# Four picks of 32 tokens in each expert gather, sums in column quarters, and copies of rows made on TensorE

## The reference, cut to what matters

```python
qh = (xb @ wq).reshape(PEER_BLOCK, PEER_HEADS, 2, PEER_DKEY // 2)        # 8 heads, 2 halves of 128
s = jnp.einsum('thcd,hckd->thck', qh, keys)                              # 128 keys for each half
sv, si = lax.top_k(s, PEER_TOPK)                                         # 16 best of each half
cand = (sv[:, :, 0, :, None] + sv[:, :, 1, None, :]).reshape(PEER_BLOCK, PEER_HEADS, -1)
cidx = (si[:, :, 0, :, None] * PEER_NKEYS + si[:, :, 1, None, :]).reshape(PEER_BLOCK, PEER_HEADS, -1)
sc, pos = lax.top_k(cand, PEER_TOPK)                                     # 16 best of 256 pairs
eidx = jnp.take_along_axis(cidx, pos, axis=-1)                           # 0 .. 16383
gw = jax.nn.softmax(sc, axis=-1)
hpre = jnp.einsum('td,thkd->thk', xb, u_tab[eidx])                       # a gathered row of u, dotted
act = jax.nn.gelu(hpre, approximate=False) * gw
return jnp.einsum('thk,thkd->td', act, v_tab[eidx])                      # gathered rows of v, weighted and summed
```

## Time and profile before

| what | value |
|---|---|
| median of 3 runs | 5446.84 us (5442.61 to 5446.93) |
| the profiled execution's own time | 5444.57 us |
| its span, granted clock | 5442.9 us, 0.932 |
| busy over the span | PE 4506.8 us (83%), DVE 2595.2 (48%), ACT 1807.0 (33%), POOL 1616.7 (30%) |
| gathers of expert rows | 1056, 1 MB each |
| DMA bytes over the span | 1639.75 MB, mean 301 GB/s |

### The profile page before, as it was taken

How to read it: one execution, slowest core, us unless ns; L and a number is a source line. 1 busy time by engine, 2 the same in 40 slices (tenths; PEclk the granted TensorE clock), 3 DMA queues, 4 the chain that set the end, 5 groups by cost and what they waited for, 6 DMA issues and landing times.

```text
span 5442.9 us, 53986 instructions
## 1 busy us (share of the span) xinstructions
PE 4506.8 (83%) x17703; PEld 2724.5 (50%) x17703; DVE 2595.2 (48%) x5453; ACT 1807.0 (33%) x4693; POOL 1616.7 (30%) x1451
## 2 busy tenths in 40 slices
PE   7999999985665666799688888888888888888898
PEld 6888888875564644344333343343333333333352
DVE  3111111115636851122266666666666666666664
ACT  3111111113323531222144444444444444444434
POOL 0000000004535820100144444444444444444433
PEclk9999999996656887899899999999999999999989
DMA  7898988751114636622499999999999999999988
GB/s 254 281 305 267 305 270 283 246 191 61 62 47 145 171 136 263 238 85 71 154 421 421 421 421 421 421 421 420 419 419 412 417 415 416 415 415 406 415 335 367
DMA packets 312486, 1639.75 MB, mean 301 GB/s; under 512 B 39384, under 2 KB 83032, under 8 KB 170328
## 3 DMA queue, kind: packets, MB, share of 16 engines
q0 software_dynamic: 167344, 1179.45, 53.1%
q1 hardware_dynamic: 109472, 235.86, 12.6%
q10 hardware_dynamic: 35456, 221.91, 12.6%
HBM read 1550.80 MB, written 315.93 MB: 343 GB/s over the span
## 4 chain that ended last, share of the span: by engine, by line
DMA 34%; PE 13%; issue 2%; ACT 1%; DVE 0%; POOL 0%; SPq 0%; DVEq 0%; POOLq 0%; ACTq 0%; PEldq 0%
DMA ex_rows<-scratch_uv,ex_E 34%; PE ex_ps_y L2353 9%; PE ex_ps_q L2322 4%; ACT ex_diag L2149 1%; ACT ex_w L2141 0%; PE ex_ps_s L2335 0%; ACT ex_gel L2137 0%; POOL ex_rows L2101 0%; SPq L2062 0%; DVE ex_dots L2275 0%; DMA ex_wq<-in_peer_wq 0%; PE ex_ps_t L2295 0%; DVE ex_rows L2275 0%; ACT ex_keysT L2108 0%; PE ex_ps_t L2306 0%
## 5 line engine op out<-in xcount | busy, mean ns | idle before, releaser
L2353 PE MATMUL ex_ps_y<-ex_rows,ex_diag 128*128 128x512 f32 (+1 forms) x4224 | 2024.9, 612 | 405.2 <-ACT ex_diag L2149 386.2
L2275 DVE CUSTOM_DVE_ANT_0 ex_rows<-ex_rows,ex_n2u 128x1024 f32<-128x1024 f32 x1056 | 1294.1, 1225 | 940.6 <-DMA ex_rows<-scratch_uv,ex_E 931.0
L2101 POOL DMA_INDIRECT ex_rows<-scratch_uv,ex_E x1056 | 1154.7, 1093 | 1724.1 <-PE ex_ps_y L2353 1491.3
L2353 PEld LDWEIGHTS ex_ps_y<-ex_rows,ex_diag 128*128 128x128 f32 (+1 forms) x4224 | 728.4, 188 | 1604.6 <-ACT ex_diag L2149 939.6
L307 PE MATMUL pj_ps<-pj_w_hi,pj_nT 128*128 128x470 f32 (+1 forms) x3456 | 783.7, 378 | 22.5 <-PE pj_ps L307 14.4
L307 PEld LDWEIGHTS pj_ps<-pj_w_hi,pj_nT 128*128 128x128 f32 (+1 forms) x3456 | 622.3, 181 | 149.3 <-issue 32.0
L2137 ACT ACTIVATE ex_gel<-ex_dots 128x1 f32<-128x1 f32 x1056 | 213.8, 202 | 1368.2 <-DVE ex_dots L2275 1367.2
L211 DVE COPY pj_zo<-pj_ps 128x470 f32<-128x470 f32 (+1 forms) x108 | 69.7, 645 | 899.4 <-PE pj_ps L307 764.6
L2149 ACT ACTIVATE ex_diag<-ex_ident,ex_w 128x128 f32<-128x128 f32 x1024 | 411.0, 401 | 50.5 <-PE ex_ps_y L2353 17.7
L307 PE MATMUL pj_ps<-pj_w_lo,pj_nT 128*128 128x470 f32 (+1 forms) x1728 | 406.0, 377 | 0.0
L211 ACT COPY pj_zo<-pj_ps 128x470 f32<-128x470 f32 (+1 forms) x108 | 59.6, 552 | 996.5 <-PE pj_ps L307 622.2
(11 more groups left out here) (351 smaller groups left out, 3925.9 us busy)
## 6 DMA issues: line engine op xcount, KB each, us to landing
pj_w<-in_w_in POOLq DMA_DIRECT2D x24, 1880.0 KB, 14.5
scratch_z<-pj_zo SPq DMA_DIRECT2D x192, 235.0 KB, 8.7
scratch_uv<-in_peer_u ACTq DMA_DIRECT2D x8, 4096.0 KB, 21.0
scratch_uv<-in_peer_v ACTq DMA_DIRECT2D x8, 4096.0 KB, 38.1
scratch_uv<-in_peer_u ACTq DMA_DIRECT2D x4, 8192.0 KB, 38.1
scratch_uv<-in_peer_v ACTq DMA_DIRECT2D x4, 8192.0 KB, 69.0
out_dk_s<-in_cache_dil_k ACTq DMA_DIRECT2D x8, 4088.0 KB, 43.6
out_dv_s<-in_cache_dil_v ACTq DMA_DIRECT2D x8, 4088.0 KB, 55.9
```

Of the source, the lines that this page charges most:

```text
L2101: pool.indirect_dma_start(out=rows[:, p % SLOTS, :], out_offset=None, in_=d["uv"], in_offset=bass.IndirectOffsetOnAxis(ap=E[:, turn % 4, k ...
L2275: nc.vector.tensor_tensor_reduce(out=row, in0=row, in1=n2u[:, tile % 2], scale=1.0, scalar=0.0, op0=ALU.mult, op1=ALU.add, accum_out=dots[ ...
L2353: last = nc.tensor.matmul(y[0:n, 512 * c:512 * c + 512], diag[:, p % DIAGS, 0:n], rows[:, p % SLOTS, D + 512 * c:D + 512 * c + 512], start ...
```

## The change

A gather of a prompt turn now takes the picks 4q to 4q+3 of 32 tokens (group g = k % 4, q = k // 4): partition 32 j + t holds pick 4q + j of token 32 g + t. The routing still computes with one token on each partition, so its results (`own`) are spread: `spread_picks` multiplies them on TensorE with four matrices `copies4`, each of which copies 32 tokens to all four blocks of partitions, and `take_spread` on DVE picks the wanted columns into `spread` and E. The dots need each group's normalised rows four times: `copy_rows` makes them on TensorE from n2r and `take_copies` copies them on ACT to `n2u`, which has four buffers and is not loaded by DMA any more. The sums use the folded 128x32 matrix in all turns, as four products of 256 columns; the product of column quarter c is written to partitions 32 c to 32 c + 31 of ps_y (column group c of TensorE). So h and y are held by column quarters and moved in four DMAs with pieces of 1 KB. `ps_y` has one buffer, and `rows` 11 slots instead of 12.

```diff
-    SLOTS = 12
+    SLOTS = 11
+    G = P // NS
+    CW = D // G
...
+        copies4 = sb("copies4", [P, G, G, NS])
-        n2r, n2u, n2T = sb("n2r", [P, D]), sb("n2u", [P, 2, D]), sb("n2T", [P, KD, P])
-        h, yo = sb("h", [P, D]), sb("yo", [P, D])
+        n2r, n2u, n2T = sb("n2r", [P, D]), sb("n2u", [P, G, D]), sb("n2T", [P, KD, P])
+        h, yo = sb("h", [P, G, CW]), sb("yo", [P, G, CW])
...
-        ps_y, ps_t = pb("ps_y", [P, 2, D]), pb("ps_t", [P, KD, P])
+        ps_y, ps_t = pb("ps_y", [P, G, CW]), pb("ps_t", [P, KD, P])
...
+        def by_column(a, tile):
+            rows32 = a[tokens(tile), :] if tile is not None else a
+            return rows32.rearrange("(g t) (c e) -> c t g e", t=NS, c=G)
...
-            def load_u(tile):
...
+            def load_h(tile):
+                n = width(tile) // NS
+                for c in range(G):
+                    sp.dma_start(h[c * NS:(c + 1) * NS, 0:n], by_column(d["h"], tile)[c]).then_inc(h_in, 16)
...
                     sp.wait_ge(n2_t, tile + 1)
+                    sp.wait_ge(copied, G * (tile + 1))
                     sp.dma_start(n2r[0:width(tile + 1)], d["n2"][tokens(tile + 1), :]).then_inc(n2r_in, 16)
-                    load_u(tile + 1)
...
+            def take_copies(tile, g):
+                act.wait_ge(copied, G * tile + g + 1)
+                if tile:
+                    act.wait_ge(dot_done, K * first_of(tile) - G + g + 1)
+                nc.scalar.copy(n2u[:, g], ps_t[:].rearrange("p k t -> p (k t)")).then_inc(n2u_out, 1)
...
             for turn in range(3):
...
                 scores(turn)
+                if turn == 0:
+                    for g in range(G):
+                        take_copies(0, g)
                 if turn < 2:
                     exponents(turn)
...
+                    if k == 0 and turn and closes(turn - 1):
+                        outputs(tile_of(turn - 1))
                     weights(turn, k)
                     diagonal(turn, k)
+                    if turn < NT * PH and closes(turn) and k >= K - G and (k - K + G) * NS < width(tile_of(turn) + 1):
+                        take_copies(tile_of(turn) + 1, k - K + G)
...
+            def take_spread(turn):
+                dve.wait_ge(r_done, turn + 1)
+                src = ps_r[:].rearrange("p (g c q j) -> p g c q j", g=G, c=2 * G, q=G)
+                for j in range(G):
+                    at = slice(j * NS, (j + 1) * NS)
+                    into = spread[at, turn % 4].rearrange("p c (q g) -> p g c q", g=G)
+                    for c in range(2):
+                        nc.vector.tensor_copy(into[:, :, c], src[at, :, c, :, j]).then_inc(spread_done, 1)
+                dve.wait_ge(spread_done, 2 * G * (turn + 1))
+                nc.vector.tensor_copy(E[:, turn % 4], spread[:, turn % 4, 0]).then_inc(E_done, 1)
...
             for turn in range(2):
                 for part in range(K):
                     route(turn, part)
+                if turn == 0:
+                    take_spread(0)
             for turn in range(TURNS):
                 for k in range(K):
                     dot(turn, k)
+                    if k == 2 and turn + 1 < NT * PH:
+                        take_spread(turn + 1)
...
+            def copy_rows(tile, g):
+                n = width(tile)
+                if tile == 0 and g == 0:
+                    pe.wait_ge(copies4_done, 1)
+                pe.wait_ge(n2T_out, tile + 1)
+                if g:
+                    pe.wait_ge(n2u_out, G * tile + g)
+                for b in range(2):
+                    last = nc.tensor.matmul(ps_t[:, 4 * b:4 * b + 4].rearrange("p k t -> p (k t)"), copies4[0:n, g].rearrange("p j t -> p (j t)"),
+                                            n2r[0:n, 512 * b:512 * b + 512], start=True, stop=True)
+                last.then_inc(copied, 1)
...
+            def spread_picks(turn):
+                if turn == 0:
+                    pe.wait_ge(copies4_done, 1)
+                pe.wait_ge(own_done, turn + 1)
+                pe.wait_ge(gate_done, turn + 1)
+                if turn:
+                    pe.wait_ge(spread_done, 2 * G * turn)
+                for g in range(G):
+                    last = nc.tensor.matmul(ps_r[:, P * g:P * g + 2 * K], copies4[:, g].rearrange("p j t -> p (j t)"),
+                                            own[:, turn % 2].rearrange("p c k -> p (c k)"), start=True, stop=True)
+                last.then_inc(r_done, 1)
...
-                for c in range(2):
-                    last = nc.tensor.matmul(y[0:n, 512 * c:512 * c + 512], diag[:, p % DIAGS, 0:n],
-                                            rows[:, p % SLOTS, D + 512 * c:D + 512 * c + 512],
+                for c in range(G):
+                    last = nc.tensor.matmul(ps_y[c * NS:(c + 1) * NS, g], diag[:, p % DIAGS, :], rows[:, p % SLOTS, D + CW * c:D + CW * (c + 1)],
                                             start=False, stop=end, skip_group_check=True)
...
             for turn in range(3):
                 if opens(turn):
                     turn_rows(turn)
+                if turn == 2:
+                    spread_picks(0)
                 queries(turn)
                 scores(turn)
+                if turn == 0:
+                    for g in range(G):
+                        copy_rows(0, g)
             for turn in range(TURNS):
                 for k in range(K):
                     sum_row(turn, k)
+                    at = k - K + G + 1
+                    if turn < NT * PH and closes(turn) and at >= 0 and at * NS < width(tile_of(turn) + 1) and at < G:
+                        copy_rows(tile_of(turn) + 1, at)
+                    if k == 1 and turn + 1 < NT * PH:
+                        spread_picks(turn + 1)
```

More of the change, by code:

```diff
@@ L2157, in outputs @@
                 if tile:
-                    act.wait_ge(y_stored, 16 * tile)
-                n = width(tile)
-                nc.scalar.copy(yo[0:n], ps_y[0:n, tile % 2]).then_inc(y_done, 1)
+                    act.wait_ge(y_stored, 16 * G * tile)
+                n = width(tile) // NS
+                nc.scalar.copy(yo[:, 0:n], ps_y[:, 0:n]).then_inc(y_done, 1)
             for turn in range(3):
@@ L2179, in _ @@
                             scores(turn + 3)
-                    if k == 3 and turn and closes(turn - 1):
-                        outputs(tile_of(turn - 1))
                     if k == 8 and turn + 2 < TURNS:
@@ L2257, in route @@
                     dve.wait_ge(pick_done, turn + 1)
-                    nc.vector.scalar_tensor_tensor(out=e, in0=picked[:, 0], scalar=float(NKEY), in1=picked[:, 1],
-                                                   op0=ALU.mult, op1=ALU.add).then_inc(E_done, 1)
+                    if turn >= 2 and turn < NT * PH:
+                        dve.wait_ge(r_done, turn - 1)
+                    into, done = (mine[:, 0], own_done) if turn < NT * PH else (E[:, turn % 4], E_done)
+                    nc.vector.scalar_tensor_tensor(out=into, in0=picked[:, 0], scalar=float(NKEY), in1=picked[:, 1],
+                                                   op0=ALU.mult, op1=ALU.add).then_inc(done, 1)
                 elif part == 14:
@@ L2274, in dot @@
                 row = rows[:, p % SLOTS, 0:D]
-                nc.vector.tensor_tensor_reduce(out=row, in0=row, in1=n2u[:, tile % 2], scale=1.0, scalar=0.0, op0=ALU.mult,
+                nc.vector.tensor_tensor_reduce(out=row, in0=row, in1=n2u[:, g], scale=1.0, scalar=0.0, op0=ALU.mult,
                                                op1=ALU.add, accum_out=dots[:, turn % 2, k:k + 1]).then_inc(dot_done, 1)
@@ L2304, in turn_rows @@
                     pe.wait_ge(n2T_out, tile)
+                    pe.wait_ge(n2u_out, G * tile)
                 for k in range(KD):
@@ L2337, in scores @@
                 last.then_inc(s_done, 1)
+            def spread_picks(turn):
[9 more added lines that the diff above has]
+                last.then_inc(r_done, 1)
             def sum_row(turn, k):
-                p, tile = turn * K + k, tile_of(turn)
-                n, y = width(tile), ps_y[:, tile % 2]
+                p, tile, g = turn * K + k, tile_of(turn), group(turn, k)
                 if k == 0 and opens(turn):
-                    pe.wait_ge(h_in, 16 * (tile + 1))
-                    if tile >= 2:
-                        pe.wait_ge(y_done, tile - 1)
-                    for c in range(2):
-                        last = nc.tensor.matmul(y[0:n, 512 * c:512 * c + 512], ident[0:n, 0:n], h[0:n, 512 * c:512 * c + 512],
+                    pe.wait_ge(h_in, 16 * G * (tile + 1))
+                    if tile:
+                        pe.wait_ge(y_done, tile)
+                    for b in range(2 if tile < NT else 1):
+                        two = slice(2 * b, 2 * b + 2) if tile < NT else slice(0, 1)
+                        last = nc.tensor.matmul(ps_y[:, two].rearrange("p g e -> p (g e)"), ident[:], h[:, two].rearrange("p g e -> p (g e)"),
```

67 lines of the change are left out of this document (32 added, 35 removed).

## The result

The changed kernel takes 5466.2 us (median of 6 runs, 5462.57 to 5470.08) against 5445.91 us for the kernel before in the same job (6 runs, 5442.61 to 5446.93): a ratio of 1.0038, 95% interval 1.0025 to 1.0051, slower by 20 us. Forecast were 5445 us, with 5466 as the upper end of the range.

What follows compares the result with a forecast made beforehand. The DMA stream of expert-row gathers, 2.49 us each at 421 GB/s, was taken as the bound. Start +10.6, bytes -6, gaps -5, tail -0.4 sum to -0.8 us: forecast 5445 us, range 5431 to 5466.

Steps and rivals of the forecast that it cites:

- the bytes: Tile loads and stores in the gather stream: n2u loads gone, h and y in 1 KB pieces; net -6 us (-9 to 0).
- the gaps: Two bursts of sample queries, queries(64) and queries(65), stop POOL's gathers: 18 us before, 13 after, -5 us (0 to -12).
- Start: Start of the experts stage: first gather waits for copies, queries(1), scores(1) and spreading; +10.6 us (8 to 21).
- the half that priced h: Loads of h and stores of y in 512 packets of 1 KB: 1.5 us each instead of 1.31, +3 us (0 to 9.6).
- The n2u half: The n2u loads of tiles 2 to 8 leave the gather stream: -7 x 1.31 = -9.2 us.
- Hidden work: Sums, spreading of picks and copies at tile ends all lie under the gathers: 0 us.
- Tail: Last landing to end: quicker sum and output copy, but four stores instead of one; -0.4 us.
- rival 1: TensorE idles more, so copies, queries and bursts run at 1.2 GHz: start +21, gaps -2; 5459 us, chance 0.13.
- Rival 2: Gather stream slows because four picks a token may read rows 1 MiB multiples apart: 2% gives 5497 us, chance 0.08.
- Rival 3: Bursts stay at 23 us or quicker catching-up shortens both gaps, -12 us: 5433 us, chance 0.17.
- rival 4: TensorE's column groups do not overlap, or tile ends starve the gather stream: 5456 us without overlap, chance 0.07.
- wrong if the stream's rate differs by over 0.5%: Sign against the forecast, which expected the gather stream at share 1.01 and 421 falling to 412 GB/s, as before.

Runs made afterwards that it cites:

- six b_ kernels: The six follow-up kernels that start from the kernel before, each with its own edits; medians from 5418.82 to 5462.27 us.
- six a_ ones: The six follow-up kernels that start from the changed kernel, each with its own edits; medians from 5436.26 to 5467.18 us.
- a_hrow: Changed kernel, h loaded as before in whole rows by one DMA over 128 partitions, column groups made on TensorE: 5451.17 us, 1.0012.
- b_h1k: Kernel before, h loaded in four DMAs of 256 columns, 1 KB pieces, each over all 128 partitions: 5447.26 us, 1.0002.
- b_hcol: Kernel before, only h loaded by column quarters: four DMAs into blocks of 32 partitions, 1 KB pieces: 5459.6 us, 1.0026.
- b_h32: Kernel before, h loaded in four DMAs of 32 partitions each, whole rows, 4 KB pieces: 5462.27 us, 1.0029.
- b_slots: Kernel before with 11 slots instead of 12: 5446.25 us, 1.0004.
- a_split: Changed kernel, the two bursts of sample queries cut into eight parts, each behind a sum: 5457.31 us, 1.0022.
- b_split: Kernel before, the two bursts of sample queries cut into eight parts, one after each of picks 4 to 11: 5425.76 us, 0.9964.
- a_pattern: Changed kernel, gathers fetching the rows of the kernel before by unspread indices, same waits, wrong outputs: 5464.45 us, 1.0034.
- a_dummy: Changed kernel plus one unread 128x512 product after each sum, to keep TensorE busier: 5467.18 us, 1.0039.

## Why the prediction was wrong

Its likeliest case was 5445 us from a sum of -0.8; measured were +20.3. Most of the error is in one term, the bytes (17 us in the traces), and 6 us are in the gaps.

- **Start, +10.6 forecast, +9.7 measured.** Right, in each link. Another 2.8 us of the profiled execution's difference lie before the stage. Over the traces the stage begins at 2660.3 to 2666.5 us in before and the six b_ kernels, and at 2664.6 to 2670.0 in the changed and the six a_ ones, means 2664.2 and 2666.7. Much of it is scatter, but a real delay of 2 us or so, whose cause no run shows, isn't excluded.
- **Bytes, -6 forecast, +10.9 measured. This is the step that failed**, in the half that priced h: "I take 1.5, near the row scaled to 1 KB: 16 x 0.19 = +3 us (0 to 9.6)". The n2u half came near: a_hrow gains 8.1 us against 9.2, though 2.8 of them with the last tile alone, whose loads go into 32 partitions. What failed was to price h and y by bytes and by the size of their pieces, when b_h1k shows no cost of the pieces. The price lies in the partitions that one DMA writes to: 2.1 to 2.2 us a tile by the dips of the rate, 14 to 17 us in all by the times of a_hrow, b_hcol and b_h32, and 18 by the dots of a_hrow and the changed kernel up to turn 61. No term and no rival had that mechanism. The upper bound of 9.6 came from a stretch of loads over all 128 partitions with no gathers beside them, and couldn't hold it.
- **Gaps, 13 us forecast for both, 19 measured.** From the dot (61, 6) to the last one, 5254.92 to 5458.57, it took 203.7 us; with the 2.49 us a gather and the loads of the forecast it would be 181.8 + 2.9 = 184.7, so 19 remain, against 18 before. The forecast took 25 us a burst; it was 27.52, all of it at 0.50, and twice 2.5 is 5 of the 6 us. b_slots puts 1 to 2 us on the slot, less than the forecast did. That the second gap would shrink because the sums are quicker didn't come: POOL idled 28.02 and 27.89 us, 24.26 and 24.16 before. The times of a_split and b_split fit a price of the clock there, without proving it.
- **Hidden work, 0 forecast, none seen.** The sums take 0.64 us at the full clock and 1.08 at the low one (forecast 0.75 and 1.3), and the clock is low for much of the stage. Spreading, diagonals and copies of the tile ends never held the stream: the share is 1.01 throughout, and b_hcol loses the same without any of them.
- **Tail, -0.4 forecast, -0.5 measured.**
- **The rivals.** Of rival 1, the low clock, the part in the gaps came true and the part in the start didn't; its 5459 us is nearer than the forecast, but for a wrong sum. Rival 2 put the slower stream on the addresses read; what slowed it was the way h was written, and a_pattern excludes the addresses. Its own evidence pointed the other way: it read the 401 GB/s of 5000:5100 as a rate that moves "with nothing else changed", while most of that fall comes with the loads of the sample tile into blocks of 32 partitions. The price of such a load stood in the trace of the kernel before. Rival 3 had the gaps closing; they grew. Of rival 4 the groups do overlap, and its lost time at the ends of tiles came as a sum, but from the loads and not from a starved stream. The sign of a falling mean, "wrong if the stream's rate differs by over 0.5%", is what happened: 413 against 417.

Start 9.7, h 14 to 18, n2u -8, gaps +1 against before, tail -0.5 make 16 to 20 of the 20.3 us. The rest is less than the intervals of the ratios, 5 to 7 us to either side, and isn't assigned.

## What to carry to other kernels

Where a DMA stream sets the time, price every other transfer not only by its bytes and pieces but by the partitions that each DMA writes: a load into 32 partitions cost its neighbours more than its own bytes did, and the DMA share of 1.01 didn't show it; the GB/s by slice and the time of a neighbour's packet did. Where a window has the full share and a lower rate, look for what else moves in it before calling the rate unsteady. Relieving an engine that isn't the bound can lower its clock, and then the one place where it is the bound, here a long burst of narrow passes, can get longer. Cutting that burst into parts between the picks, in the kernel before, gained 20 us, as much as the rebuilt stage lost.

## What the runs showed of the hardware

- Four loads of 128 KB, each into 32 partitions, lowered the rate of a gather stream beside them from 421 to about 355 GB/s for 12.5 us (1 KB pieces) or to about 290 for 6 us (4 KB pieces), 2.1 and 2.2 us lost. Stores from the same blocks left it at 274 ns a packet.
- Pieces of 1 KB over 128 partitions cost no more than pieces of 4 KB: 1.0002 [0.9993, 1.0011].
- TensorE fully busy with passes of 32 moving columns stayed at a granted clock of 0.50 through both bursts of 27.52 us. With wider work before them, in a_dummy, the same bursts took 24.60 and 21.77 us.
- Eight passes of 256 columns in four column groups take 0.64 us at the full clock, against 1.92 us for four passes of 512 columns: the groups do overlap.
